# A single decoder step on one core: GpSimd's key products wait for the rotary embedding, three key sums move behind the first prompt units, and one gate tile is cut in two

## The reference, cut to what matters

```
h = RMSNorm(x);  h @ w_in  ->  A: q,k,v | B: q (3 groups), k, v | C: q | gate logits (3 x 1024)
A  sliding-window attention with sinks, partial rotary (rope)
B  dilated attention: keys at distances 0,d,2d,.. for (128,1),(512,4),(2048,16), partial rotary
C  cross-attention into 256 memory tokens
merged = sum over branches of sigmoid(gate_i) * (o_i @ w_br_i);   x = x + merged @ w_out
x = x + top-4-of-32 mixture of experts(RMSNorm(x));   y = RMSNorm(x)
```

## Time and profile before

| | |
|---|---|
| median of 3 runs | 1279.67 us (1278.82 to 1281.4) |
| profiled execution, its own time | 1280.43 us |
| its span in the trace | 1278.6 us |
| PE busy | 1211.9 us, 95% of the span |
| DVE / ACT / POOL busy | 421.9 / 233.9 / 74.7 us |
| moved by the transfers | 502.37 MB |

### The profile page before, as it was taken

How to read it: one execution, slowest core, us unless ns; L and a number is a source line. 1 busy time by engine, 2 the same in 40 slices (tenths; PEclk the granted TensorE clock), 3 DMA queues, 4 the chain that set the end, 5 groups by cost and what they waited for, 6 DMA issues and landing times.

```text
span 1278.6 us, 14751 instructions
## 1 busy us (share of the span) xinstructions
PE 1211.9 (95%) x6107; PEld 513.6 (40%) x6122; DVE 421.9 (33%) x919; ACT 233.9 (18%) x459; POOL 74.7 (6%) x79
## 2 busy tenths in 40 slices
PE   9998999999999999999999999999999999899996
PEld 4456667666533333333333333333333333233332
DVE  3275643325442313223142322313131413222233
ACT  2211534230210112101112010111011110101012
POOL 0480002400200000000000000000000000000000
PEclk9998999999999999999999999999999999999998
DMA  9999999889799999999999999999999999999994
GB/s 339 386 305 337 307 359 358 269 274 421 281 391 387 430 429 426 428 427 428 427 429 427 428 430 427 427 428 428 428 426 430 427 427 429 427 428 429 429 426 178
DMA packets 74792, 502.37 MB, mean 393 GB/s; under 512 B 6992, under 2 KB 31184, under 8 KB 49104
## 3 DMA queue, kind: packets, MB, share of 16 engines
q1 hardware_dynamic: 72864, 497.10, 96.0%
q0 software_dynamic: 848, 2.36, 0.6%
q10 hardware_dynamic: 1008, 1.90, 0.4%
HBM read 498.42 MB, written 37.03 MB: 419 GB/s over the span
## 4 chain that ended last, share of the span: by engine, by line
PE 61%; DMA 31%; DVE 5%; SPq 2%; issue 1%; ACT 1%; DVEq 0%; ACTq 0%
PE ps L1803 20%; DMA ring<-in_w_gate_up 17%; PE ps L1842 10%; DMA late<-in_w_gate_up 7%; DMA tail<-in_w_gate_up 7%; PE ps L1190 5%; PE ps L1274 5%; PE ps L1759 3%; PE ps L1703 3%; PE ps L1553 2%; PE ps L1566 2%; PE ps L1820 1%; PE ps L1320 1%; PE ps L1722 1%; PE ps L1441 1%
## 5 line engine op out<-in xcount | busy, mean ns | idle before, releaser
L1803 PE MATMUL ps<-ring,cq 128*64 128x512 f32 x1232 | 283.4, 602 | 22.0 <-DMA ring<-in_w_gate_up 22.0
L1803 PEld LDWEIGHTS ps<-ring,cq 128*64 128x64 f32 x1232 | 84.5, 138 | 195.3 <-issue 146.0
L1842 PE MATMUL ps<-ring,cq 128*64 128x512 f32 x592 | 134.3, 595 | 0.7 <-issue 0.7
L1274 PE MATMUL ps<-arena,ring 128*128 128x288 f32 x384 | 104.3, 418 | 2.0 <-ACT ring L933 2.0
L2338 DVE TENSOR_REDUCE tail<-ps 128x1 f32<-128x288 f32 x15 | 6.9, 458 | 290.3 <-PE ps L1735 290.3
L1074 ACT ACTIVATE cq<-ps 128x512 f32<-128x512 f32 x32 | 19.1, 597 | 450.8 <-PE ps L1820 450.8
L1274 PEld LDWEIGHTS ps<-arena,ring 128*128 128x128 f32 x384 | 70.7, 192 | 26.0 <-issue 4.9
L1842 PEld LDWEIGHTS ps<-ring,cq 128*64 128x64 f32 x592 | 41.0, 136 | 73.3 <-issue 69.8
L2366 DVE TENSOR_TENSOR x_tok<-x_tok,ps 64x512 f32<-64x512 f32 (+2 forms) x51 | 43.9, 860 | 67.1 <-PE ps L1759 61.6
L1190 PE MATMUL ps<-ring,arena 128*128 128x512 f32 (+1 forms) x192 | 64.2, 598 | 1.1 <-DMA ring<-in_w_in 1.0
L1088 ACT ACTIVATE cq<-ps 64x512 f32<-64x512 f32 x32 | 18.9, 590 | 230.4 <-PE ps L1842 230.4
(11 more groups left out here) (390 smaller groups left out, 1320.5 us busy)
## 6 DMA issues: line engine op xcount, KB each, us to landing
ring<-in_w_gate_up SPq DMA_DIRECT2D x77, 2048.0 KB, 42.6
ring<-in_w_down SPq DMA_DIRECT2D x37, 2048.0 KB, 43.9
tail<-in_w_gate_up SPq DMA_DIRECT2D x13, 2048.0 KB, 41.1
late<-in_w_gate_up SPq DMA_DIRECT2D x12, 2048.0 KB, 42.3
cq<-in_w_gate_up SPq DMA_DIRECT2D x12, 2048.0 KB, 42.8
arena<-in_w_gate_up SPq DMA_DIRECT2D x12, 2048.0 KB, 42.8
ring<-in_w_in SPq DMA_DIRECT2D x9, 2048.0 KB, 13.2
out_dil_k_s<-in_cache_dil_k SPq DMA_DIRECT2D x8, 2044.0 KB
```

What stands on the lines that cost most here:

```text
L1274: ins = pe.matmul(bank(gate_bank(m))[:, 0:TT], wblk[AREA[6 + m // 4]][:, k, (m % 4) * P:(m % 4 + 1) * P], hT_v[:, k, :], start=(k == 0), s ...
L1803: ins = pe.matmul(bank(gu0 + u)[64 * h:64 * h + 64, :], xTe[:, k % 4, (k // 4) * 64:(k // 4) * 64 + 64], pair_buf[slot][:, a:a + 512], sta ...
L1842: ins = pe.matmul(bank(7 if last else 5)[64 * h:64 * h + 64, :], aT[:, kk % 4, (kk // 4) * 64:(kk // 4) * 64 + 64], pair_buf[slot][:, a:a ...
```

## The change

GpSimd waits for all six ropes before the products of sequence 6 (and so of 7). `sum_keys(5)` leaves its place behind the ropes; sums 5, 6 and 7 now stand behind prompt units 0, 1 and 2, where sums 6 and 7 stood behind units 0 and 1. Gate tile 20 is opened after tile 19 and the first half of its products is issued before the wait for `s_p_ready`, the second half where the whole tile stood. No arithmetic is added or removed.

```diff
             for b in range(NB_S):
 
                 pool.wait_ge(*keys_in(b))
+                if b == 6:
+                    pool.wait_ge(S["rope_done"], 6)
                 if b == 7:
                     pool.wait_ge(S["q_rep_in"], 16 * 2 * NQ_S)
...
             gate_tile()
             gate_tile()
             gate_tile()
+            gate = gate_open()
+            gate_products(gate, range(KC // 2))
 
             pe.wait_ge(S["s_p_ready"], 1)
...
             for g in range(3):
                 if g == 2:
-                    gate_tile()
+                    gate_products(gate, range(KC // 2, KC))
                     pe.wait_ge(S["s_pt_evicted"], 1)
...
                 rope(t, kv[0:r, t, 0:384], 6, "rope_done")
-            sum_keys(5)
             for n in range(TR_Q):
                 evict_tr(TR_H + n, TR_H + n)
...
-            SUMS_BEHIND = (0, 1)
+            SUMS_BEHIND = (0, 1, 2)
...
                 if u in SUMS_BEHIND:
-                    sum_keys(6 + SUMS_BEHIND.index(u))
+                    sum_keys(5 + SUMS_BEHIND.index(u))
```

## The result

The changed kernel takes **1271.74 us** (median of 5 runs, 1271.22 to 1274.05) against 1279.67 (5 runs, 1277.52 to 1281.4): a ratio of 0.994, with a 95% interval of 0.9928 to 0.9957. The profiled execution took 1272.24 us, its span is 1270.4. The forecast was 1271.1.

The account below looks back on a forecast made before the run. PE holds 61% of the chain and VectorE is no bound, so VectorE edits pay only where PE waits. Gains of 6.75 + 1.8 = 8.55 us, taken from the median of 1279.67, give 1271.1 us; range 1269.5 to 1272.5, chance 0.70.

Parts of the forecast that it names:

- Edits 1 and 2: Rope stage: GpSimd waits for ropes (1), sum 5 leaves (2); PE's 4.05 us gap and 2.7 of clock go: 6.75 us.
- 3 us of slack: Rope stage: of VectorE's 8.3 us freed, about 3 are slack, as PE's first query transposes come only at 99.45 us.
- Copies: VectorE's evictions out of PSUM beside GpSimd's products: no cost taken, under 0.3 us in all as far bound.
- Rival B: Rope stage: GpSimd's products shut out copies out of PSUM, the first ending at 109.4; 1281.8 us in all. Chance 0.03.
- Edit 3: Sums 5, 6, 7 behind prompt units 0, 1, 2: unit 4 starts 0.2 us late; cost nothing, at most 0.2.
- the queue was full: SP's queue: the dot keys, released at 139.85, only stand in a queue that is full anyway; transfers finish some 6 us earlier.
- Rival A: SP's queue: dot keys' release doesn't move, PE waits 2.1 us for block 10: 1273.2 us. Chance 0.14.
- Edit 4: Half of gate tile 20 before the probability transposes fills PE's 2.25 us idle time: 2.03 - 0.2 = 1.8 us.
- rival A's loss of clock: Behind PE's wait for block 10 the clock falls too, 2.7 us more: 1275.9 us.
- told 8.55: Whole kernel: the 6.75 us of the rope stage plus 1.8 of the split tile.

Follow-up runs that it names:

- The gap put back: Changed kernel plus three, in a second kernel four, extra VectorE reductions of sum 5's size behind the ropes: 1276.59 us and 1279.9 us.
- the late release: Changed kernel with sum 7 behind unit 4 instead of unit 2, so the dot keys are released later: 1274.26 us, ratio 0.9958.
- the split alone: Kernel before the change with only gate tile 20 issued in two halves: 1278.96 us, ratio 0.999.
- The wait alone: Kernel before the change with only GpSimd's products of sequences 6 and 7 waiting for the ropes: 1275.51 us, ratio 0.9962.
- the kernel with the moved sums: Kernel before the change with only sums 5, 6, 7 moved behind units 0, 1, 2: 1276.18 us, ratio 0.997.
- the wait and the split: Changed kernel with sum 5 back behind the ropes and sums 6 and 7 behind units 0 and 1: 1273.35 us, ratio 0.9947.
- second set: The changed kernel measured once more, no edit: 1271.55 us against 1279.11 for the kernel before, ratio 0.9947.
- the bias loads: The wait alone, with GpSimd's bias loading and splitting held until s_p_ready: 1276.17 us; with sums 6 and 7 behind units 0 and 2 too: 1275.39 us.

## Why the prediction was right, step by step

**Edits 1 and 2, 6.75 us: measured 7.03.** The mechanism is the one told. PE reaches the second group at 101.33 (told: 101.46). The next three steps take 105.46 - 101.33 = 4.13 us (told: 4.26, from steps of 1.42; one of them has three transposes and takes 1.31). These two differences of 0.13 are the surplus. The ropes end at 96.45 and the first product starts at 96.59 (told: 96.45 and 96.5). The gap put back shows that the two terms belong together: 5.11 us of gap cost another 2.01 us of clock.

The 3 us of slack were right, and the statement that edits 1 and 2 free 8.3 us of which much is slack holds more sharply than I put it: edit 1 alone makes the gap zero, so edit 2 is worth nothing beside it, though it is worth 3.25 us without it.

**Copies, cost nothing: right.** 0.69 us beside the products, at 101.97. Rival B rested on this. It is also where the Trainium skill was weighed: "SBUF - State Buffer", section "Who interferes with whom", names copies in a two-port mode among what a GpSimd instruction shuts out; "VectorE: DVE Perf Modes", section "Why PSUM operands drop a tier", takes copies out of PSUM from it. The runs agree with the two together: two-input ropes at 1.39 against 0.31 us, copies out of PSUM not slowed.

**Edit 3, cost at most 0.2 us: measured 0.07.** DVE's and SP's timelines of the changed kernel, against the earlier trace rows, the line of the gate blocks, against the earlier trace rows, and PE's first half of gate tile 16, against the earlier trace rows:

```profile
137.24 2.28 DVE L1987 TENSOR_REDUCE h_tok<-ring 128x32 f32<-128x2048 f32 x1
139.44 0.55 DVE L2042 TENSOR_TENSOR late<-ps,arena 128x384 f32<-128x384 f32 x1
```

```profile
139.55 0.35 SPq L553 DMA_DIRECT2D tail<-in_cache_dil_k  x1
...
179.76 0.59 SPq L507 DMA_DIRECT2D ring<-in_w_in  x1
```

```profile
DMA to landing us min/median/max: 10.7/10.7/10.7
```

```profile
195.31 2.11 PE L1276 MATMUL ps<-arena,ring 128*128 128x288 f32 x8
```

Unit 4 starts at 139.44; 146.37 less the 7.0 us by which the scores came earlier is 139.37. PE doesn't feel it: "units" is 84.97 in both kernels. The release of the dot keys came at 139.55 (told: 139.85), so it did stand still while PE moved up. The value loads in front moved up 5.75 us, from 124.01 to 118.26 (told: some 6; SP is still issuing stores until then). Block 10 moved up 6.5 us, landed at 179.76 + 10.7 = 190.5, and was used at 195.31: 4.8 us of slack, as the 4.7 before. Why the unmoved release does no harm is seen at the third sequence's dot keys, on SP's queue before and after:

```profile
142.59 9.63 SPq L553 DMA_DIRECT2D tail<-in_cache_dil_k  x1
```

```profile
142.35 3.95 SPq L553 DMA_DIRECT2D tail<-in_cache_dil_k  x1
```

Before, SP was held at this issue for 9.6 us, until 152.2; now for 4.0, until 146.3. It waits 7.2 us for the release instead of 1.5, and is held 5.7 us less behind it. In the kernel without the moved sums the release comes at 133.28 and the same issue takes 10.96 us, until 147.1; in the one with the late release, at 149.04, it takes 0.47. So a release anywhere from 133 to 140 us does not set the time of what follows; the queue was full, as told. What ended the hold, the profile doesn't say. Rival A fell, and the run with the late release shows it wasn't a bad rival: its wait at tile 16 begins when the release comes 9.5 us later.

**Edit 4, 1.8 us: measured 2.01 - 0.37 = 1.64** in the changed kernel, and 1.64 alone. The cost is 0.37 us and not 0.2. The step left out is the time from the end of ACT's eviction of tile 19 to PE's start, which I had put at nothing. ACT's timeline of the changed kernel:

```profile
232.58 0.41 ACT L935 ACTIVATE ring<-ps 128x288 f32<-128x288 f32 x1 [2.89 <-PE ps L1276]
```

It ends at 232.99, PE starts at 233.13, 0.14 us later (0.15 with the split alone).

**What was argued wrongly**, though the sum didn't rest on it: against rival A's loss of clock I said that a gap of 2.25 us does no harm. The wait alone has 2.58 us in the same place and loses 1.6 us to the clock; the kernel with the moved sums has 1.93 at the ropes and loses 1.85. So edit 4 can be worth more than told beside edit 1. In the profiled executions "rows" and "pT" together are 24.05 us with the wait alone and 20.47 in the changed kernel, 3.6 us; with the kernel before they are 22.11, and 20.47 with the split alone. By the medians it is 1275.51 against 1273.35 us (the wait and the split), 2.2. Why the gaps of 2.25 and 3.12 us left the clock at 1.00 is open.

**The end.** "Rest" is between 1000.9 and 1002.4 us in all the kernels run: the experts' stream starts earlier by what the front gained, and its length stays. The SP wait for the attention's last eviction is 5.3 us (5.6 before). 8.53 - 0.33 = 8.2 us on the span; told 8.55. The edited stages gave 7.03 + 1.64 = 8.67; that the total comes so near is in part luck, since three stages that no edit touches differ by 0.3 to 0.4 us each ("values" +0.30, "keys" -0.41, "rest" -0.33). The medians differ by 7.93 and, in the second set, 7.56 us; the start's wandering by 2 us lies inside these.

## What to carry to other kernels

Look at what two engines do to each other only where a third one waits, and take the clock into the price of a gap: here 1.9 to 5.1 us of idle PE cost another 1.6 to 3.0 us behind it in most cases, and nothing in two. Try every edit alone and with the one it overlaps: the moved sums were worth 3.25 us alone and nothing beside the wait, the split tile 1.6 alone and, in the profiled executions, 3.6 beside it. Before work is moved away from an engine it disturbs, its transfers have to be placed too; the bias loads gave back all that the softmax gained.

## What the runs showed of the hardware that was not expected

- The clock fell behind gaps of 1.93, 1.99, 2.58, 2.79, 4.05, 4.70 and 5.11 us, and not behind 1.57, 2.25 and 3.12. It isn't the length alone that decides, and no run here shows what does. The 5.11 us gap cost less clock (2.01 us) than the one of 4.05 (2.98), since more of the low stretch lay inside it. Behind 1.93 and 2.79 us the first instructions after the gap could still be at full clock (0.63 us for four transposes at 103.36 and 104.26, the normal 0.60), and the fall came about a microsecond later.
- Small two-input VectorE instructions take four times as long and more beside GpSimd: 128x128 takes 1.20 us beside GpSimd's subtractions and 0.29 alone; 128x160 takes 1.39 beside its products and 0.31 alone. The large copies out of PSUM (128x512) take 0.69 us with or without company.
- With 12 loads of 64 KB on GpSimd's queue beside them, the value loads on SP's queue landed after 8.0 and 8.5 us (two kernels). In the other kernels they took 2.9 to 5.8 us, so they vary a good deal by themselves.
